# Four of eight expert blocks with at most 64 rows: both halves side by side, two matmul passes in place of three

## The reference

```python
logits = (xt @ router_w).astype(jnp.float32)
top_v, top_e = lax.top_k(logits, TOP_K)          # TOP_K = 2, N_EXPERTS = 8
gate = jax.nn.softmax(top_v, axis=-1)
...
return (jax.nn.silu(xblk @ w1[e]) * (xblk @ w3[e])) @ w2[e]
```

## Time and profile before

| | |
|---|---|
| median of 3 runs | 1989.75 us (1989.38 to 1990.35) |
| span of the profiled execution, first to last instruction | 1986.5 us |
| from the start of the expert blocks to the end of the span | 1016.4 to 1986.5 us |
| one expert block of the loop (1129.70 to 1249.02 us) | 119.32 us |
| PE, DVE, ACT busy in the whole span | 99%, 82%, 65% |
| granted TensorE clock, mean | 0.999 |

### The profile page before, as it was taken

The page is one execution under the profiler, slowest core; times in us unless marked ns, Lnnn a source line. Parts: engine busy times, 40 slices in busy tenths (PEclk is TensorE's granted clock), DMA queues, the critical chain, the costliest instruction groups (busy, mean ns, idle before and its releaser), DMA issues.

```text
span 1986.5 us, 31923 instructions
## 1 busy us (share of the span) xinstructions
PE 1969.3 (99%) x12185; PEld 1767.6 (89%) x12185; DVE 1638.9 (82%) x1702; ACT 1288.2 (65%) x1155; POOL 46.3 (2%) x89
## 2 busy tenths in 40 slices
PE   9999999999999999999999999999999999999998
PEld 8999999989999999999988888888888888888886
DVE  6999967577778988976578888988989888888986
ACT  7666555444436666564467777878778787777775
POOL 0000000000000000000000000000000000000000
PEclk9999999999999999999999999999999999999999
DMA  8545556445555545555479999999999999999994
GB/s 269 171 133 184 166 173 199 143 160 194 192 176 170 170 133 170 191 182 186 136 290 382 374 381 384 361 385 358 388 379 369 381 362 385 372 380 385 359 392 170
DMA packets 311377, 533.26 MB, mean 268 GB/s; under 512 B 14363, under 2 KB 157363, under 8 KB 311271
## 3 DMA queue, kind: packets, MB, share of 16 engines
q1 hardware_dynamic: 308550, 523.71, 74.8%
q0 software_dynamic: 2720, 8.08, 1.5%
HBM read 526.30 MB, written 7.34 MB: 269 GB/s over the span
## 4 chain that ended last, share of the span: by engine, by line
PE 88%; DVE 6%; ACT 2%; issue 2%; SPq 1%; DMA 0%; DVEq 0%; ACTq 0%
PE ps L1898 26%; PE ps L1900 26%; PE ps L1899 26%; PE ps L2213 4%; DVE w_lo L1214 2%; PE ps L2215 2%; ACT w_hi L764 1%; PE ps L2317 1%; DVE c L1281 1%; PE ps L2067 1%; PE ps L2087 1%; DVE xf L1299 0%; PE ps L2399 0%; PE ps L2033 0%; SPq L511 0%
## 5 line engine op out<-in xcount | busy, mean ns | idle before, releaser
L1214 DVE TENSOR_TENSOR w_lo<-raw,w_hi 128x2048 fp32r<-128x2048 f32 (+1 forms) x330 | 745.2, 2260 | 190.4 <-ACT w_hi L764 131.1
L1898 PE MATMUL ps<-w_hi,a_hi 128*128 128x512 f32 (+1 forms) x1472 | 568.0, 386 | 1.1 <-DVE w_lo L1214 1.1
L1900 PE MATMUL ps<-w_hi,a_lo 128*128 128x512 f32 (+1 forms) x1472 | 560.8, 381 | 0.0
L1899 PE MATMUL ps<-w_lo,a_hi 128*128 128x512 f32 (+1 forms) x1472 | 559.8, 380 | 0.0
L1898 PE MATMUL ps<-a_hi,w_hi 128*128 128x256 f32 x1456 | 416.2, 286 | 2.0 <-DVE a_lo L1569 1.6
L1899 PE MATMUL ps<-a_lo,w_hi 128*128 128x256 f32 x1456 | 411.9, 283 | 0.0
L1900 PE MATMUL ps<-a_hi,w_lo 128*128 128x256 f32 x1456 | 411.8, 283 | 0.0
L771 ACT ACTIVATE w_hi<-raw 128x2048 fp32r<-128x2048 f32 x168 | 322.3, 1919 | 119.8 <-PE ps L1900 119.2
L764 ACT ACTIVATE w_hi<-raw 128x2048 fp32r<-128x2048 f32 x157 | 296.3, 1894 | 56.7 <-PE ps L1900 52.1
L1898 PEld LDWEIGHTS ps<-w_hi,a_hi 128*128 128x128 f32 x1472 | 276.7, 188 | 54.5 <-DVE w_lo L1214 3.7
L1900 PEld LDWEIGHTS ps<-w_hi,a_lo 128*128 128x128 f32 x1472 | 276.5, 188 | 53.8
(11 more groups left out here) (357 smaller groups left out, 2313.3 us busy)
## 6 DMA issues: line engine op xcount, KB each, us to landing
raw<-in_moe_w SPq DMA_DIRECT2D x168, 1024.0 KB, 7.0
raw<-in_w_in SPq DMA_DIRECT2D x66, 1024.0 KB, 5.2
mem_t<-in_moe_w SPq DMA_DIRECT2D x56, 1024.0 KB, 6.8
area<-in_moe_w SPq DMA_DIRECT2D x56, 1024.0 KB, 6.9
xf<-in_moe_w SPq DMA_DIRECT2D x56, 1024.0 KB, 6.7
raw<-in_ffn_w SPq DMA_DIRECT2D x33, 1024.0 KB, 5.3
raw<-in_w_mlstm_out SPq DMA_DIRECT2D x8, 1024.0 KB, 5.1
raw<-in_w_out SPq DMA_DIRECT2D x8, 1024.0 KB, 5.9
```

The lines of the kernel that those rows point to most:

```text
L1214: return dve.tensor_tensor(dst, whole, as_f32(hi), ALU.subtract)
L1898: pe.matmul(dst, wh, xh, start=start, stop=False, skip_group_check=True)
L1899: pe.matmul(dst, wh, xl, start=False, stop=False, skip_group_check=True)
L1900: return pe.matmul(dst, wl, xh, start=False, stop=stop, skip_group_check=True)
```

## The change

The block order is decided at run time. Block 0 stays expert 0. `plan`, new on DVE behind the route, ranks the seven other experts by their rows and gives the four smallest to "light" blocks and the three largest to "heavy" ones; the order of blocks is heavy, light, heavy, light, heavy, light, light, heavy (`KINDS`). SP reads the expert of blocks 1 to 7 from the table `ids`. A light block takes at most 64 rows; an expert whose rows overflow its block gets a further heavy block behind the eighth. With the rows above none does.

Heavy blocks are as before. In a light block the hi and the lo half of the 64 rows stand side by side in one stationary operand of 128 columns (`x_both`, `hid_both`), so a chunk is 4 x 2 matmuls of 512 columns: both halves by `w_hi`, both by `w_lo` (which also adds lo by lo). A product then has two halves on partitions 0 to 63 and 64 to 127, which must be added. ACT copies both products of a group out of PSUM (`l_copied`), and eight fp32 matmuls with `fold` (two stacked identities of 64) turn them and add the halves in one go (`turn_fold`); silu, product and split then work on 256 columns in place of 512. At a light block's end ACT copies the upper half of the result, DVE adds the lower, ACT scales it, for each 512 columns. Each step of a light block splits the weights first and does its own work after, as in a heavy one.

The core of the diff (left out: the renamed constants' semaphore, the landing semaphores shared with the layers before, the caps of 64 in `further_blocks`, the 64-row form of the indirect add, the outer loops of the other engines, `gather_lo`, and the `w2` half of `l_chunk`):

```diff
 SLOTS = 128
-N_OVER = (2 * T - 1) // (SLOTS + 1)
+LIGHT = 64
+KINDS = "HLHLHLLH"
+N_LIGHT = KINDS.count("L")
+N_PAIRS = 3
+N_OVER = 4
...
+        x_both = flat2(b_lo)[:, D:2 * D].rearrange("p (k i s) -> p k i s", k=KB, i=2)
+        hid_both = [flat2(a_hi)[:, D + i * FG:D + (i + 1) * FG].rearrange("p (k i s) -> p k i s", k=4, i=2) for i in range(2)]
+        up_copy, gate_copy = ([flat2(t)[:, i * FG:(i + 1) * FG] for i in range(2)] for t in (cacc, c31))
...
+            sp.wait_ge(ids_done, 1)
+            with sp.Fori(1, NE - 1) as b:
+                e = expert_of(b)
+                for m in range(N_EXP):
+                    expert_load(b, m, e)
...
+                    if "L" in kinds:
+                        src = ps[banks[i]][:, :].rearrange("p (k s) -> p k s", k=4)[:, :, 0:LIGHT]
+                        ins = act.activation(x_both[:, 4 * i:4 * i + 4, 0, :], src, ACT.Copy)
...
+            def l_post(b, j, m, kinds):
+                kind, g, i = ESEQ[m]
+                if m == N_EXP - 1:
+                    for n, done in enumerate((y_half.at(b, 1), None)):
...
+                        act.activation(y_low[:, n * 512:(n + 1) * 512], ps[4 + n][LIGHT:P, :], ACT.Copy).then_inc(l_copied.sem, 1)
+                    for n in range(2):
+                        c = slice(n * 512, (n + 1) * 512)
+                        act.wait_ge(l_y_sum.sem, l_y_sum.at(j, n + 1))
+                        act.activation(y_rows[0:LIGHT, c], y_low[:, c], ACT.Copy, scale=gate_col[0:LIGHT, :]).then_inc(ye_done.sem, 1)
+                    return
+                act.wait_ge(e_pe.sem, e_pe.at(b, m + 1))
+                if kind != "w2" and i == 1:
+                    if g >= 2:
+                        act.wait_ge(e_turned.sem, e_turned.at(b, g - 1))
+                    dst = (up_copy, gate_copy)[kind == "w3"]
+                    act.activation(dst[g % 2], ps[(2 * g + (kind == "w3")) % 4][:, :], ACT.Copy).then_inc(l_copied.sem, 1)
+                turned = {E_AT["w1", n + 1, 1]: n for n in range(NGE - 1)} | {E_AT[TURN_LAST]: NGE - 1}
+                if m in turned:
+                    n = turned[m]
+                    act.wait_ge(e_turned.sem, e_turned.at(b, n + 1))
+                    act.activation(act_l[n % 2], ps[6][:, 0:T], ACT.Silu).then_inc(e_silu.sem, 1)
+                    act.wait_ge(e_gated.sem, e_gated.at(b, n + 1))
+                    act.activation(hid_both[n % 2][:, :, 0, :], act_l[n % 2].rearrange("p (k s) -> p k s", k=4), ACT.Copy).then_inc(e_hid_hi.sem, 1)
+                if (kind, g, i) == ("w3", 1, 1):
+                    act.wait_ge(rows_read.sem, rows_read.at(b, 4))
...
+            def l_block(b, j, kinds):
+                for t in range(SPL, N_EXP + SPL):
+                    first = ESEQ[t - SPL] in POST_FIRST
+                    if first:
+                        l_post(b, j, t - SPL, kinds)
+                    if t < N_EXP:
+                        e_split(b, t)
+                    if not first:
+                        l_post(b, j, t - SPL, kinds)
+                    if t >= N_EXP:
                         e_split(b + 1, t - N_EXP)
 
...
                     act.activation(f_tile[1][:, c], f_tile[1][:, c], ACT.Copy, scale=f_stat[3][:, 1:2]).then_inc(f_act.sem, 1)
 
-            with act.Fori(0, NE - 1) as b:
-                e_block(b)
+            with act.Fori(0, N_PAIRS) as i:
+                e_block(2 * i)
+                l_block(2 * i + 1, i, "HL")
+            l_block(NE - 2, N_PAIRS, "H")
...
+            def l_post(b, j, m, kinds):
+                if m == N_EXP - 1:
+                    for n in range(2):
+                        c = slice(n * 512, (n + 1) * 512)
+                        dve.wait_ge(l_copied.sem, l_copied.at(j, 2 * NGE + n + 1))
+                        dve.tensor_tensor(y_low[:, c], y_low[:, c], ps[4 + n][0:LIGHT, :], ALU.add).then_inc(l_y_sum.sem, 1)
+                    return
+                dve.wait_ge(e_pe.sem, e_pe.at(b, m + 1))
+                turned = {E_AT["w1", n + 1, 1]: n for n in range(NGE - 1)} | {E_AT[TURN_LAST]: NGE - 1}
+                if m in turned:
+                    n = turned[m]
+                    dve.wait_ge(e_silu.sem, e_silu.at(b, n + 1))
+                    dve.tensor_tensor(act_l[n % 2], act_l[n % 2], ps[6][:, T:2 * T], ALU.mult).then_inc(e_gated.sem, 1)
+                    dve.wait_ge(e_hid_hi.sem, e_hid_hi.at(b, n + 1))
+                    lo(hid_both[n % 2][:, :, 1, :], act_l[n % 2].rearrange("p (k s) -> p k s", k=4), hid_both[n % 2][:, :, 0, :]).then_inc(e_hid_lo.sem, 1)
+                next_rows(b, m, kinds)
...
+            def plan():
+
+                ch.link(dve.tensor_copy(total, ps[5][:, 32:32 + NE]))
+                ch.link(dve.scalar_tensor_tensor(key, total, float(NE), iota8, ALU.mult, ALU.add))
+                ch.link(dve.tensor_scalar(key[:, 0:1], key[:, 0:1], 0.0, -1.0, ALU.mult, ALU.add))
+                mine = key.rearrange("p (e o) -> p e o", o=1).broadcast_to([P, NE, NE])
+                other = key.rearrange("p (o e) -> p o e", o=1).broadcast_to([P, NE, NE])
+                ch.link(dve.tensor_tensor(beats, mine, other, ALU.is_gt))
+                ch.link(dve.tensor_reduce(place, beats, AX, ALU.add))
+                at = place_of.rearrange("p (b o) -> p b o", o=1).broadcast_to([P, NE, NE])
+                of = place.rearrange("p (o e) -> p o e", o=1).broadcast_to([P, NE, NE])
...
+                which = chosen.rearrange("p (o b) e -> p o b e", o=1).broadcast_to([P, 1 + 3 * TT, NE, NE])
+                ch.link(dve.tensor_tensor(picked, each, which, ALU.mult))
+                ch.link(dve.tensor_reduce(by_block[:, :, 1:NE], picked[:, :, 1:NE, :], AX, ALU.add))
+                dve.tensor_copy(ids[0:1, 1:NE], ids_f[0:1, 1:NE]).then_inc(ids_done, 1)
...
+            def turn_fold(b, j, g):
+
+                pe.wait_ge(l_copied.sem, l_copied.at(j, 2 * g + 2))
+                if g:
+                    pe.wait_ge(e_gated.sem, e_gated.at(b, g))
+                for n, src in enumerate((up_copy, gate_copy)):
+                    for k in range(4):
+                        c = n * T + k * LIGHT
+                        ins = pe.matmul(ps[6][:, c:c + LIGHT], src[g % 2][:, k * P:(k + 1) * P], fold[:, :],
+                                        start=(n == 0 and k == 0), stop=True, skip_group_check=True)
+                ins.then_inc(e_turned.sem, 1)
...
+                    for k in range(4):
+                        c = slice(k * FG, (k + 1) * FG)
+                        both, dst = x_both[:, 4 * i + k, :, :].rearrange("p i s -> p (i s)"), ps[(2 * g + up) % 4][:, :]
+                        pe.matmul(dst, both, wh[:, c], start=(i == 0 and k == 0), stop=False, skip_group_check=True)
+                        ins = pe.matmul(dst, both, wl[:, c], start=False, stop=(i == 1 and k == 3), skip_group_check=True)
+                ins.then_inc(e_pe.sem, 1)
...
+            def l_block(b, j):
+                for m, (kind, g, i) in enumerate(ESEQ):
+                    l_chunk(b, j, m)
+                    if m == ROWS_AT:
+                        slot_rows(b + 1, ps[7][:, 0:3])
+                    if kind == "w1" and i == 1 and g:
+                        turn_fold(b, j, g - 1)
+                    if (kind, g, i) == TURN_LAST:
+                        turn_fold(b, j, NGE - 1)
+                    if (kind, g, i) == ("w2", NGE - 2, 1):
+                        turn_rows(b)
```

196 lines of the change are left out of this document (137 added, 59 removed).

## The result

The changed kernel takes 1999.64 us (median of four runs, 1997.0 to 2004.05) against 1989.57 us before (1987.73 to 1990.35): a ratio of 1.0056, with a 95% interval of 1.0042 to 1.007. It is slower by 10 us, where 4.4 us less were forecast. The profiled execution is the slowest of the four, 2002.3 us of span against 1986.5.

The account below looks back on a forecast made before the run. PE, busy for 99% of the span, was taken as the limit, with DVE limiting light blocks after the change. Light blocks -6.0 and plan() +1.6 gave -4.4 us: 1989.75 to 1985.3 us, range 1972 to 2000.

Parts of the forecast that it names:

- the light blocks: Each of four light blocks takes 117.8 us at DVE's pace against 119.3 before: -6.0 us in all.
- plan(): Eight new DVE instructions ahead of chunk 3's split in block 0, 2.75 us long, stall PE: +1.6 us (0.5 to 3).
- the heavy blocks: PE's and ACT's heavy blocks stay as they are, 119.3 us each: 0.
- dearer round trip: Rival: short product and hi part cost as much as on 512 columns, 13.7 us over 28 groups, 1999.0 us; chance 0.15.
- the loads: Rival: DMA loads set the pace at 2.80 us a chunk, nothing is saved, 1993.8 us; chance 0.12.
- The long step: The step of a light group with DVE's product and ACT's hi part: 4.93 us, DVE idle for 2.1.
- the light block's end: Adding the halves takes DVE 1.2 us, then it waits 2.5 us for ACT's scaling and next weight split.
- the covered waits: Rival: ACT gets ahead, DVE needs 100.6 us a light block, DMA limits at 113: -23.6, 1966 us; chance 0.12.
- the ninth block: Rival: a light expert has more than 64 rows, so a further block comes: +119 us, 2105 us; chance 0.03.
- Clock 1.00 throughout: PE keeps the upper clock of 2.4 GHz in light blocks despite gaps up to some 2 us: nothing in the sum.
- The Trainium skill's rule: Rival: PE's short bursts in light blocks drop it to 1.2 GHz, 157 us a block, +152, 2142 us; chance 0.08.

Follow-up runs that it names:

- the straight version: The changed kernel with its loops over the expert blocks written out on every engine: 1992.09 us, ratio 1.0014.
- heavy pairs: The kernel before with two heavy blocks per turn of its loops on ACT, DVE, PE and SP: 1996.01 us, ratio 1.0036.
- short fillers: 6, 8 and 11 unused PE matmuls at light blocks' ends, added to the straight version: 1989.59 us; with result late and steps handed out too: 1987.13 us.
- straight, with the result late and the steps handed out: The straight version, next block's third chunk split before a light block's result, table steps one per chunk in block 0 and the last block: 1987.22 us, ratio 0.999.

## Why the prediction was wrong

The sum had three terms: -6.0 us for the light blocks, +1.6 for plan(), and 0 for the heavy blocks. By the medians of the runs ACT's loop is worth 8.3 us that the sum did not have; the tables cost 3.0 in place of 1.6; and with ACT's loop out of the way the four light blocks gain 1.1 in place of 6.0. That is -4.4 + 8.3 + 1.4 + 4.9 = +10.2 us, and +10.1 were measured. (Each of these differences can be off by 1 to 3 us.) The time lies just inside the stated range of 1972 to 2000 us. That is luck: the upper end of the range was there for a dearer round trip and for the loads, and neither came.

**The light block: right inside, too cheap at its end.** The long step is 4.89 us (4.93 forecast), and a group 15.9 to 16.1 (15.93) where no other work of DVE falls into it. ACT waits 1.9 us for DVE's product, DVE waits 2.6 us at the light block's end (2.5). The loads are hidden, if narrowly: ACT waits for landings 3.7 us in a light block, 0.6 each time, while six chunks at the forecast's 2.64 us are 15.84 of a group's 15.93. The block's pace is DVE's. Of the rivals the dearer round trip, the loads, the covered waits and the ninth block are out; the time came out near the first of them, for none of its reasons.

But the forecast gain is hardly there. A light block behind a light one (interval 6) was to take 117.8 us and takes 120.72 in the changed kernel, 119.65 in the straight version, 118.21 with ACT's loop alone written out. A light and a heavy interval together were to take 117.8 + 119.3 = 237.1; they take 240.6 and 239.0 in the straight version, 237.35 and 237.70 with ACT's loop out (its profiled execution is the fastest of its eleven), against 238.6 before. The step of the prediction that was short is the light block's end: it put DVE's wait of 2.5 us there and nothing for PE, which stands idle there, so that the next block begins with matmuls at the lower clock: 8 of them behind blocks 1 and 3 in the straight version (from 1263.43 and 1495.37), 0.2 us more each, some 1.6 us as an estimate. The end is where the loss can be won back: with the third chunk split ahead of the result, four light blocks are worth 4.4 us (1988.01 against 1992.44). How the rest divides between the clock and the waits is open.

**The step that failed most: "PE's and ACT's heavy blocks stay as they are: 0".** The code of a heavy block is the same, its surroundings are not. Two blocks stand in one turn of the loop now. At the turn's end ACT has no instruction for 3.1 us, then loads a table for 1.28, and DVE's fourth chunk waits 4.0 us for it, at both jumps. A second table load follows ahead of the first silu, and DVE waits 1.0 us more behind that. Writing out ACT's loop alone takes 8.3 us off, in a kernel that lost 10.1; the same edit in the kernel before takes off 0.8, within the noise. This is shown. Before, the jump had the same two table loads and no gap, and they were covered: DVE waited 0.7 and 1.4 us and PE, as the limit, had chunks to work on. A light block's end takes such cover away, since there ACT sits 3 us in a wait for DVE ahead of its last split and PE has run dry. What the jump waits for is only argued. ACT's loop body has 153 instructions in the kernel before and 346 now, counted in the built programs with the waits, PE's has 625 and 1105. The profile's row of the instruction queue has 100 packets of 16.4 KB now (1.64 MB) against 73, but that is no sign of the gap: it has 100 with ACT's loop written out as well.

```profile
q8 instruction: 100, 1.64, 0.3%
```

The Trainium skill (Runtime: NRT & Kernel Launch, Instruction fetch mechanics) says that an engine holds two pages of 256 instructions (2048 instructions on PE), fetches ahead in a line only, and has to fetch again when a branch goes to a page that it no longer holds. The traces agree in part. The two gaps of ACT stand behind the jump and go with it, and PE's waits for issue of over 2 us come with the long bodies (2.6 us with heavy pairs, 4.7 here, 0.2 before). The count does not agree: 346 instructions are fewer than two pages of 256, PE's bodies of 1105 and 1248 (heavy pairs) fewer than 2048, and all three waited, while ACT's body of 301 with heavy pairs did not. So the length of the body alone does not decide, and what does is open.

**plan(): right in itself, +1.6; the start as a whole was not.** Its eight new steps from 1023.28 to 1025.91 are 2.6 us (2.75 forecast), and PE waits 1.47. But the first transposes come 3.45 us later than before: PE's first chunk is itself late by 1.9 us (1018.36), of which the clock, 0.79 from 1010 to 1018 in this execution, is a part. In the profiles of the version with ACT's loop written out it is 1.00 (first transposes at 1131.64), in that without light blocks 0.81 and 0.76 (1132.74), with the same steps. A late start need not come from the change: the kernel before with two blocks per turn and the kernel before with ACT's loop written out have the old code up to there, a clock of 0.79 in that stretch all the same, and their first transposes at 1131.21 and 1130.47 in place of 1129.54.

**A term that the sum lacked: further_blocks().** Its caps of 64 make it 0.93 us longer, in front of the last block, where it was exposed already. PE's gap there is 2.08 us in place of 1.07, and it is followed by the lower clock. All-heavy code with these tables is 3 us slower than the kernel before; in its profile the last interval is 2.4 us longer.

**The clock: its place wrong.** In the changed kernel's light intervals it is 1.00, as forecast: bursts with gaps of up to 1.6 us between them do not lower it there. The fall comes at the blocks' joints: 0.54 at 1257.3, behind a gap of 4.3 us, and 0.51 at 1742.1, behind two gaps of 1.57 and 1.95 us with 2.1 us of matmuls between them. "Clock 1.00 throughout" was wrong. The Trainium skill's rule (TensorE: Matmul & The Clock Gate, HAM oscillation — how this bites in real kernels) was put down for the bursts, where the trace disagrees; at 1257.3, behind the longest gap, it agrees, and at 1742.1 the gaps are shorter than the waits of the page's example. What the clock costs in the changed kernel no run prices. In the straight version the short fillers bring 2.5 us, at the edge of the noise and net of their own cost.

**The sum in the profiles.** From the forecast of -4.4 us to the profiled execution: each of the two pairs of intervals with a jump is 243.0 in place of 237.1 us, 11.8 together, of which 11.0 go with ACT's loop out; the start is 1.85 more than plan()'s 1.6; the last three intervals are 383.3 us where 379.7 - 3.0 = 376.7 were forecast, 6.6 more, of which 2.1 stay with ACT's loop out. That gives +15.9, against a measured +15.8 of the spans (the medians differ by 10.1: this execution lies 4.4 us above its kernel's median). The 11.0 are too much for ACT's loop, since the slowest of four executions stands here against the fastest of eleven (4.0 us under its median): 16.8 us of span apart, where the medians say 8.3. Against the profile of the straight version, which is 1.2 us above its median, the same four intervals differ by 6.4. For the same reason the 4.5 us by which the last three intervals are longer with ACT's loop than without, though ACT has no jump back in them, may be scatter; what the profile shows there is the lower clock (0.51 at 1742.1).

## What to carry to other kernels

A loop body that is made longer by pairing two blocks can have a price at the jump back (6.9 us with two heavy blocks, on PE; 8.3 us here, on ACT). Look at what each engine waits for just ahead of the jump before trusting that "the rest stays as it is", and try the loop written out on each engine that shows an issue gap: here both ACT and PE showed one, and only ACT's cost time. Price an exposed joint for every engine, not only for the one that waits there. When an engine with 99% of the span is relieved, a short series of small instructions on the new limit (here 2.6 and 3.4 us of tables) becomes visible. Handing it out one per step took PE's gap away in block 0 and 2.1 us off the last stretch; in the medians the gain is within the noise. The versions that are straight, with the result late and the steps handed out (0.999, and 0.9986 with short fillers) are the first below the kernel before, by some 2 us. Saving one matmul pass in three in half of the blocks is worth no more, because a light block then goes at DVE's pace, at best 118 us where PE's was 119.3, and by the forecast's estimate the loads stand 4% behind that.

## What was not expected of the hardware

- ACT without any instruction for 3.1 us, and 4.8 us with nothing between the result and the jump, and 6.2 and 6.1 us from the release of its last wait to the table load behind the jump.
- The table loads of 1.28 us at the head of ACT's loop body and ahead of its first silu are there only with the loop; written out, the blocks have none, and ACT goes on at 1.81 us from split to split.
- A single gap of 2.23 us on PE, in an otherwise full heavy block, was followed by eight matmuls at the lower clock (from 1500.27 with heavy pairs); one of 1.86 us in the same kernel was not.
- The clock at the start of the expert blocks (1010 to 1018 us) is 1.00 in some executions and 0.67 to 0.9 in others of nearly the same code, and where it is low, everything behind it comes 0.9 to 1.7 us later in the kernels without new tables. The kernels with light blocks scatter over 5 to 8 us from run to run (1987.32 to 1994.62 with ACT's loop out), the kernel before over 3.
- PE's weight loads wait for issue some 25 us in the light blocks of straight code (up to 4 us of it reach PE's matmuls), and 16 us with PE's loop kept, and neither shows in the time.
